# DVE's order in the mixed attention stage of a two-block fp32 kernel: attended sum and convolution passes on the other side of an exponent

## What is computed

```python
def stick_breaking_attention(q, k, v):        # 8 heads of 64, 1024 tokens
    ...
        z = jnp.einsum("bhqd,bhkd->bhqk", qb, kb).astype(jnp.float32) * scale
        strict = s_idx < t_idx
        log_keep = jnp.where(strict, jax.nn.log_sigmoid(-z), 0.0)
        later = lax.cumsum(log_keep, axis=3, reverse=True) - log_keep
        w = jnp.where(strict, jnp.exp(jax.nn.log_sigmoid(z) + later), 0.0)
        outs.append(jnp.einsum("bhqk,bhkd->bhqd", w, vb.astype(jnp.float32)))

def second_block(x, ...):
        h = rms_norm(x, norm_mix_pre[l])
        proj = h @ w_in[l]
        q, k, v, cb, cc, cx, g_att, g_conv = jnp.split(proj, IN_SPLITS, axis=-1)
        o = stick_breaking_attention(heads(q), heads(k), heads(v))
        y_att = o.transpose(0, 2, 1, 3).reshape(b, s, ATT_WIDTH) @ w_att_branch[l]
        y_conv = (cb * causal_dwconv(cc * cx, conv_mix_w[l])) @ w_conv_branch[l]
        merged = jax.nn.sigmoid(g_att) * y_att + jax.nn.sigmoid(g_conv) * y_conv
        x = x + rms_norm(merged @ w_out[l], norm_mix_post[l])
        ...                                    # gated feed-forward part with another convolution
```

## Time and profile before

| | |
|---|---|
| median of 3 runs | 2136.54 us (2134.32 to 2136.9) |
| the profiled execution | 2131.11 us |
| its span, first to last instruction | 2129.2 us |
| PE busy with matmuls in the span | 2083.3 us (98%) |
| DVE, ACT, POOL busy | 1085.8, 826.7 and 748.2 us |
| mean granted clock of TensorE | 0.998 |

### The profile page before, as it was taken

How to read it: one execution, slowest core, us unless ns; L and a number is a source line. 1 busy time by engine, 2 the same in 40 slices (tenths; PEclk the granted TensorE clock), 3 DMA queues, 4 the chain that set the end, 5 groups by cost and what they waited for, 6 DMA issues and landing times.

```text
span 2129.2 us, 27902 instructions
## 1 busy us (share of the span) xinstructions
PE 2083.3 (98%) x10634; PEld 1736.2 (82%) x10634; DVE 1085.8 (51%) x1570; ACT 826.7 (39%) x1478; POOL 748.2 (35%) x661
## 2 busy tenths in 40 slices
PE   7999999999999999999999999999999999999998
PEld 7988889998787787878878888878888888878786
DVE  5574668886271766757667551632222322222613
ACT  4341269996142554635456421522221222121211
POOL 2532422223234222222322435043323333266673
PEclk9999999999999999999999999999999999999999
DMA  5212110101232121212122542421111111132432
GB/s 164 67 47 73 62 63 11 51 11 46 90 128 61 41 75 44 74 35 74 55 58 79 193 149 99 149 70 41 48 49 49 49 40 49 49 109 89 158 107 99
DMA packets 144828, 159.92 MB, mean 75 GB/s; under 512 B 6955, under 2 KB 112967, under 8 KB 144727
## 3 DMA queue, kind: packets, MB, share of 16 engines
q1 hardware_dynamic: 121319, 97.45, 15.0%
q10 hardware_dynamic: 23408, 61.10, 8.2%
HBM read 129.16 MB, written 29.36 MB: 74 GB/s over the span
## 4 chain that ended last, share of the span: by engine, by line
PE 86%; DVE 8%; ACT 3%; issue 2%; DMA 1%; ACTq 0%; POOL 0%; SPq 0%; DVEq 0%
PE psum L678 19%; PE psum L680 18%; PE psum L679 18%; PE psum L1042 15%; PE psum L938 3%; PE psum L950 3%; PE psum L1079 1%; PE psum L969 1%; PE psum L970 1%; PE psum L971 1%; DVE softplus_part L2268 1%; PE psum L1096 1%; PE psum L688 1%; PE psum L1063 1%; PE psum L1095 1%
## 5 line engine op out<-in xcount | busy, mean ns | idle before, releaser
L570 POOL TENSOR_TENSOR w_ring<-w_staging,zero 128x8 fp32r<-128x8 f32 x172 | 50.1, 291 | 1163.7 <-PE psum L680 695.2
L573 POOL TENSOR_TENSOR w_ring<-w_staging,w_ring 128x1024 fp32r<-128x1024 f32 (+1 forms) x172 | 439.7, 2556 | 14.4
L1042 PE MATMUL psum<-h,w_ring 128*128 128x512 f32 x1728 | 430.5, 399 | 0.7 <-ACT v L1582 0.7
L1042 PEld LDWEIGHTS psum<-h,w_ring 128*128 128x128 f32 x1728 | 314.6, 188 | 67.1 <-ACT v L1582 1.1
L678 PE MATMUL psum<-ffn_in,w_ring 128*128 128x512 f32 x672 | 265.4, 395 | 0.0
L680 PE MATMUL psum<-ffn_in,w_ring 128*128 128x512 f32 x672 | 264.3, 393 | 0.0
L679 PE MATMUL psum<-ffn_in,w_ring 128*128 128x512 f32 x672 | 263.8, 393 | 0.0
L2401 DVE SCALAR_TENSOR_TENSOR up_buf<-psum,vectors,up_buf 128x1023 f32<-128x1023 f32 x44 | 56.5, 1283 | 309.6 <-ACT up_buf L1825 309.6
L571 POOL TENSOR_SCALAR w_ring<-w_staging 128x1016 fp32r<-128x1016 f32 (+1 forms) x172 | 185.0, 1075 | 0.0
L1825 ACT ACTIVATE up_buf<-psum,vectors 128x1024 f32<-128x1024 f32 x44 | 49.2, 1117 | 268.0 <-PE psum L680 267.9
L680 PEld LDWEIGHTS psum<-ffn_in,w_ring 128*128 128x128 f32 x672 | 126.0, 187 | 30.4
(11 more groups left out here) (297 smaller groups left out, 4556.3 us busy)
## 6 DMA issues: line engine op xcount, KB each, us to landing
w_staging<-in_w_in SPq DMA_DIRECT2D x58, 512.0 KB, 3.8
w_staging<-in_w_up SPq DMA_DIRECT2D x44, 512.0 KB, 3.8
w_staging<-in_w_down SPq DMA_DIRECT2D x44, 512.0 KB, 3.3
w_staging<-in_w_out SPq DMA_DIRECT2D x16, 512.0 KB, 3.8
scratch_gates<-gate_out ACTq DMA_DIRECT2D x32, 256.0 KB, 2.5
merge_gates<-scratch_gates ACTq DMA_DIRECT2D x16, 512.0 KB, 4.5
x_again<-scratch_x ACTq DMA_DIRECT2D x16, 512.0 KB, 4.3
x_again<-in_x ACTq DMA_DIRECT2D x16, 256.0 KB, 2.7
```

What stands on the lines that cost most here:

```text
L573: pool.tensor_tensor(lo[:, 0:width], WS[:, s, 0:width], plain(hi[:, 0:width]), ALU.subtract).then_inc(S["w_split"], 1)
L1042: ins = pe.matmul(mix_bank(h), (sl if x == 2 else sh)[:, P * k:P * k + P], ml if x == 1 else mh, start=m == 0, stop=m == UNIT // 2 - 1)
```

## The change

DVE's loop over the steps takes two things later. The convolution pass that belongs to step i was the last but one thing of step i, behind the attended sum and ahead of `exponent(i + 1)`; now it stands behind `exponent(i + 1)`. The attended sum of an odd step moves in the same way, but only where the next step has at most four key tiles (`late_sum`): this holds for the steps 11, 13, 15, 17, 27, 29, 31, 33, 43, 45, 47, 49, 59 and 61. In the other odd steps it stays. Nothing is added or removed, and the semaphores that each instruction waits for and raises are as they were. The order of PE, ACT and SP, the matmuls and the transfers are the same.

```diff
+            def late_sum(i):
+                return i >= 3 and i % 2 and i < STEPS - 1 and stick_width(i + 1) <= 4
+
...
             for i in range(STEPS + 1):
                 if i < STEPS:
                     exponent(i)
+                if late_sum(i - 1):
+                    attended2((i - 4) // 2)
+                if i - 1 in PASSES:
+                    conv_pass(*PASSES[i - 1])
                 if i in BORDERS:
                     evacuate((i, 0))
                 if i:
...
                 evacuate((i, 1))
                 if i:
                     weights_lo(i - 1, 1)
-                if i >= 3 and i % 2:
+                if i >= 3 and i % 2 and not late_sum(i):
                     attended2((i - 3) // 2)
                 evacuate((i, 2))
-                if i in PASSES:
-                    conv_pass(*PASSES[i])
```

## The result

The changed kernel takes 2122.09 us (median of 6 runs, 2119.66 to 2124.35), the kernel before 2135.14 us (6 runs, 2131.82 to 2136.9): ratio 0.9941, with a 95% interval of 0.9930 to 0.9951. The profiled executions differ by less: 2131.11 and 2124.35 us.

The account below looks back on a forecast made before the run. PE was taken as the bound, busy 2083.3 of 2129.2 us, so only its idle time could be won. Waits of 3.7 + 2.29 + 2.22 = 8.2 us, with costs 0, took 2136.54 to 2128.3 us; range 2125.0 to 2134.0 us.

Parts of the forecast that it names:

- both long ones: PE's waits for the exponent at steps 2 and 33, 2.29 and 2.22 us, both to be won whole.
- The predicted 0.06 us at step 2: The scan would ask 0.06 us before POOL's L571 ends, and so go ahead of L573.
- the first rival: Scan misses the gap at a long wait: 2130.3 us if at step 2, 2132.2 us if at both; chance 0.20.
- the term that is won: PE's nine waits (L1063) for the exponent vanish: seven small ones 3.7 us, two long 2.29 and 2.22, sum 8.2 us.
- the seven small waits: PE's shorter waits for the exponent, counted as 3.7 us and all to be won.
- Cost (2): Deferred work delays `weights_lo` at steps 12, 28, 44, 60 and 6: bounds 0 and 4.8 us, taken as 0.
- the back-to-back argument: At step 12 DVE has no pause: exponent 0.91 us sooner, sum follows, `weights_lo` again at 790.3; cost nothing.
- the third line of waits: PE's transposes (L1079) waiting for `weights_lo`, seven times, 2.2 us; expected to stay within 0.5 us.
- the difference off the median: The profiled execution lay 5.4 us below the median; 8.2 us off the median 2136.54 gave 2128.3 us.
- the delayed `weights_lo`: Rival: the 4.8 us of deferred work ahead of `weights_lo` are paid, 3.4 us won, 2133.1 us; chance 0.12.
- nothing to be measured: Rival: ACT's soft part or PE's own order holds the exponent, the waits stay, 2136.5 us; chance 0.08.
- slower: Rival: deferred passes stand still for L573 ahead of `weights_lo`; seven blocked whole give 2147.2 us; chance 0.04.

Follow-up runs that it names:

- after: The changed kernel's first run, against the kernel before: 2122.09 us, ratio 0.9941.
- after_again: The changed kernel run a second time with no edit, against the kernel before: ratio 0.9952, first to last L1065 461.7 us.
- passes_only: Only the 24 convolution passes move behind the exponent, attended sums stay; against the kernel before: ratio 0.9949, first to last L1065 463.1 us.
- pass5_stays: The changed kernel with the pass of step 5 back at its old place: first to last L1065 460.7 us.
- hybrid: The changed kernel, with the sums in steps 12, 28, 44, 60 and the pass in step 6 behind `weights_lo`: 2117.58 us, ratio 0.9926 to the kernel before.
- lo_first: The changed kernel with all deferred sums and passes behind `weights_lo` instead of ahead: ratio 0.9961 to the kernel before, first to last L1065 464.8 us.
- nudge: The changed kernel with two tiny memsets ahead of `exponent(2)`, no wait for their end: first to last L1065 461.7 us.
- nudge_linked: The changed kernel with two tiny memsets ahead of `exponent(2)`, each with a wait for its end: first to last L1065 465.6 us.

## Why the prediction was wrong in size

- **The direction and the mechanism were right.** The nine waits of the matmuls for the exponent are gone, both long ones included. At these two it is because the scan takes the pass's place in the gap between L571 and L573. The predicted 0.06 us at step 2 measured 0.07 us in the changed kernel, and asking 0.3 us later than that brought 1.98 us of wait back, where the first rival had put 2.0 us.
- **The step that failed is the term that is won**, "Sum: 3.7 + 2.29 + 2.22 = 8.2 us". It took the idle time of the matmuls for what a wait costs, and the times at which "PE was ready" with it. The weight loads' list gives 11.4 us before and 0.6 us after, 10.8 us, and the length of the stage agrees to 0.1 us in after, after_again, passes_only and pass5_stays. That is 2.6 us more than the term; 2.0 of them belong to the seven small waits, 5.7 us where the sum had 3.7. In hybrid and lo_first, where waits for `weights_lo` go whole, the list is off by about a microsecond.
- **What the prediction left out**: the clock behind the two long waits. With the 10 of 19 measured it is about 2 x 0.53 x 1.6 = 1.7 us on average, and nothing in an execution in which it does not fall, as in the one profile I had. The clocks of all executions on record bear the size out: the mean granted clock was 0.9968 over the 35 executions of the kernel before that stand beside the experiments and 0.9975 over ten of the changed kernel. 0.0007 of 2135 us is 1.5 us, an estimate that is uncertain by some 0.5 us.
- **Cost (2) was taken as 0 and is 0.6 us net.** At steps 12, 28, 44 and 60 the back-to-back argument held (weight loads' wait 0.89 after 0.99 us, 0.87 after 1.00, 0.29 after 0.41 and 0.28 after 0.26). At step 6 it did not, since I asked only whether the pass fits in time and not what POOL does then: 0.9 us. The pass took 1.58 us there, more than the 1.18 us that the bound allowed for it. So the third line of waits, named as a sign (2.2 us within 0.5 us), came to 2.8 us.
- **The profiled execution against the median.** Working from the difference off the median kept the 5.4 us between them. By the estimate above 1.7 us of them are this clock term, which the change takes away; the rest is scatter of the one execution.
- Sum of what was found: 10.8 - 0.6 + 1.7 = 11.9 us, ratio 0.9944. The two measurements are 0.9941 (0.9930 to 0.9951) and 0.9952 (0.9937 to 0.9966); the sum lies in both intervals. Whether the clock term is 1.0 or 2.2 us can't be told from 19 cases.
- Rivals: the delayed `weights_lo` came true at one place of five; "nothing to be measured" and "slower" did not. The deferred passes did meet L573 at steps 2 and 33 (2.23 and 2.37 us long), hidden as forecast.

## What to carry to other kernels

Size a wait of TensorE by the idle time of its weight loads and check it by the length of the stage between two fixed matmuls, which decides. The matmuls' idle time was too low here (8.2 us where 10.8 were won); the loads' was right for the waits for the exponent and 0.23 us too high for each wait for `weights_lo` that went whole. Before moving an instruction behind another on VectorE, ask for each place what GpSimd runs at that moment and whether the instruction takes its tensors from SBUF alone: moved into the wrong tenth of a microsecond it stands still for a whole GpSimd instruction. Put deferred work where the engine was idle, and ahead of what another engine already waits for only if nothing can block it. Look at the granted clock behind each longer wait of TensorE, since a fall makes it dearer than it looks, and profile a kernel more than once before taking one execution's span as typical.

## What the runs showed of the hardware

- In the mixed stage the granted clock fell to 0.50 (1.2 GHz) beside 10 of 19 waits with the weight loads idle for 2.1 us or more, and beside none of 1.85 us and less. It stayed there for about 3 us in nine cases and for about 7 us at the wait of 4.67 us, and cost about 1.6 us each time, 2.5 us at that one. Elsewhere in the program it fell beside 11 of 14 waits of 2.6 us, and in two profiles beside one of 1.45 us. The Trainium skill (TensorE: Matmul & The Clock Gate, section Part 1: The HAM clock gate) has two levels for the clock, the lower one for an engine that was idle. The rows above agree with the two levels, and each of these falls stands beside a wait; that it comes with only some waits of one length is what the runs add.
- DVE's scan and pass with two SBUF operands against POOL's instructions: which asks first goes first, for the whole instruction, and a DVE instruction that is already waiting gets through between two POOL instructions that follow each other. Asking 0.04 us before the end was enough (nudge), 0.13 us after the start of the next was not (nudge_linked). DVE instructions with one operand in PSUM ran beside POOL unharmed: the 33 L2280 of the kernel before that overlap a POOL instruction take as long as those of their size that don't.
- Two operands in SBUF are not needed for it. The first tap, L2320, reads one tensor from SBUF and writes to SBUF; alone it takes 0.48 us. In the changed kernel it meets L571 once, and ends 0.27 us after it:

```profile
726.83 1.04 POOL L571 TENSOR_SCALAR w_ring<-w_staging 128x1016 fp32r<-128x1016 f32 x1
727.16 0.98 DVE L2320 TENSOR_SCALAR conv_y<-cc_cx,vectors 128x512 f32<-128x512 f32 x1
```

In lo_first it meets L573 and takes 1.99 us. In the changed kernel nothing on PE waited for it.
